# Two transformer blocks on one core: paced attention units, the renormalised residual on GpSimd, and feature turns ahead of the squares

## Time and profile before

| | us |
|---|---|
| median of 3 (range) | 2647.72 (2647.49 to 2649.39) |
| the profiled execution | 2649.36 |
| its span | 2647.6 |
| TensorE busy | 2628.9 |
| VectorE busy | 1698.8 |
| ScalarE busy | 1155.3 |
| GpSimd busy | 7.4 |

### The profile page before, as it was taken

How to read it: one execution, slowest core, us unless ns; L and a number is a source line. 1 busy time by engine, 2 the same in 40 slices (tenths; PEclk the granted TensorE clock), 3 DMA queues, 4 the chain that set the end, 5 groups by cost and what they waited for, 6 DMA issues and landing times.

```text
span 2647.6 us, 34571 instructions
## 1 busy us (share of the span) xinstructions
PE 2628.9 (99%) x12676; PEld 2209.8 (83%) x12676; DVE 1698.8 (64%) x2521; ACT 1155.3 (44%) x1549; POOL 7.4 (0%) x43
## 2 busy tenths in 40 slices
PE   9999999999999999999999999999999999999999
PEld 7978888888878888888888888888888888888887
DVE  7668764566767555655565687877755555555555
ACT  5333444534344444444444644454444444444443
POOL 0000000000000000000000000000000000000000
PEclk9999999999999999999999999999999999999999
DMA  7545556555545556655566566544566555555555
GB/s 229 180 153 173 152 160 222 191 191 174 186 141 185 191 188 189 194 191 188 189 194 207 177 199 183 155 139 144 163 198 191 190 190 190 190 190 190 190 190 167
DMA packets 262501, 483.67 MB, mean 183 GB/s; under 512 B 17738, under 2 KB 39172, under 8 KB 262020
## 3 DMA queue, kind: packets, MB, share of 16 engines
q1 hardware_dynamic: 262372, 482.37, 57.4%
q10 hardware_dynamic: 32, 0.01, 0.0%
HBM read 480.22 MB, written 2.10 MB: 182 GB/s over the span
## 4 chain that ended last, share of the span: by engine, by line
PE 95%; DVE 3%; ACT 1%; issue 0%; DMA 0%; SPq 0%; ACTq 0%; DVEq 0%
PE bank L1087 26%; PE bank L1089 25%; PE bank L1088 25%; PE bank L1045 4%; PE bank L1048 4%; PE bank L1046 4%; PE bank L1175 2%; PE bank L1138 1%; DVE w_split L1257 1%; PE bank L1208 1%; PE bank L1191 1%; PE bank L1185 0%; PE bank L1210 0%; ACT act_junk L845 0%; ACT w_split L859 0%
## 5 line engine op out<-in xcount | busy, mean ns | idle before, releaser
L859 ACT ACTIVATE w_split<-w_raw 128x1024 fp32r<-128x1024 f32 (+2 forms) x920 | 960.7, 1046 | 1226.1 <-PE bank L1089 977.9
L1257 DVE TENSOR_TENSOR w_split<-w_raw,w_split 128x1024 fp32r<-128x1024 f32 (+2 forms) x920 | 1088.4, 1203 | 431.0 <-ACT w_split L859 422.0
L1087 PE MATMUL bank<-w_split,act_a 128*128 128x512 f32 (+2 forms) x1888 | 738.1, 391 | 3.7 <-DVE w_split L1257 2.5
L1089 PE MATMUL bank<-w_split,act_a 128*128 128x512 f32 (+2 forms) x1888 | 724.0, 383 | 0.0
L1088 PE MATMUL bank<-w_split,act_a 128*128 128x512 f32 (+2 forms) x1888 | 722.8, 383 | 0.0
L1087 PE MATMUL bank<-w_split,act_b_hi 128*128 128x512 f32 x1240 | 485.8, 392 | 1.3 <-issue 1.0
L1089 PE MATMUL bank<-w_split,act_b_lo 128*128 128x512 f32 x1240 | 482.9, 389 | 0.0
L1088 PE MATMUL bank<-w_split,act_b_hi 128*128 128x512 f32 x1240 | 482.6, 389 | 0.0
L1087 PEld LDWEIGHTS bank<-w_split,act_a 128*128 128x128 f32 x1888 | 354.7, 188 | 70.6 <-DVE w_split L1257 3.5
L1089 PEld LDWEIGHTS bank<-w_split,act_a 128*128 128x128 f32 x1888 | 354.4, 188 | 67.7
L1088 PEld LDWEIGHTS bank<-w_split,act_a 128*128 128x128 f32 x1888 | 354.9, 188 | 63.6
(11 more groups left out here) (209 smaller groups left out, 1238.8 us busy)
## 6 DMA issues: line engine op xcount, KB each, us to landing
w_raw<-in_w_ff SPq DMA_DIRECT2D x256, 512.0 KB, 4.0
w_raw<-in_w_in SPq DMA_DIRECT2D x208, 512.0 KB, 3.8
w_raw<-in_w_gate SPq DMA_DIRECT2D x88, 512.0 KB, 4.1
w_raw<-in_w_up SPq DMA_DIRECT2D x88, 512.0 KB, 4.5
w_raw<-in_w_down SPq DMA_DIRECT2D x88, 512.0 KB, 4.6
w_raw<-in_w_out SPq DMA_DIRECT2D x64, 512.0 KB, 4.4
w_raw<-in_w_in SPq DMA_DIRECT2D x24, 368.0 KB, 3.3
w_raw<-in_w_dsa_o SPq DMA_DIRECT2D x16, 512.0 KB, 4.9
```

Source lines behind the costliest of these rows:

```text
L859: nc.scalar.activation(whi[:, s, 0:w], raw[:, s, 0:w], ACT.Copy).then_inc(hi_ready, 1)
L1087: pe.matmul(o, x_hi, rhs_hi, start=k == 0, stop=False)
L1089: ins = pe.matmul(o, x_lo, rhs_hi, start=False, stop=k == c["kt"] - 1)
L1257: v_e.tensor_tensor(wlo[:, s, 0:w], raw[:, s, 0:w], whi[:, s, 0:w].bitcast(F32), ALU.subtract).then_inc(lo_ready, 1)
```

## The change

The change has three parts.

1. A new function `paced_attention` stands in for `attention` in DSA, MoBA and FoX (the memory attention keeps the old one), and `nsa_attention` has the new order too. A unit's steps are now [P of u-2, S of u, O of u-3] in one place and [N of u] by itself in the next.
2. The four `renorm` steps go from VectorE to GpSimd: for each half of the tokens one multiplication by the row factor and one by the gains. GpSimd waits for all norms so far and for the gains, with the first of them alone. A new step `renormed`, at the second chunk of `vf`, makes VectorE wait for all four.
3. In the weaves of `mo[2]` and `mo[3]` the turns `hf[0:2]` and `hf[2:4]` come ahead of the squares, which puts them one group earlier.

```diff
--- before.py
+++ after.py
@@ -168,21 +168,36 @@
     return out, values
 
 
-def nsa_attention(units):
+def paced_attention(units):
 
     out, m, values = [], len(units), []
-    for i in range(m + 1):
-        one, two = [], []
-        if i >= 1:
-            one.append(("N", units[i - 1]))
-            two.append(("P", dict(unit=units[i - 1], slot=(i - 1) % 3)))
+    for i in range(m + 3):
+        one = []
+        if 2 <= i < m + 2:
+            one.append(("P", dict(unit=units[i - 2], slot=(i - 2) % 3)))
         if i < m:
             one.append(("S", units[i]))
-        if i % 3 == 1 and i > 1:
-
-            values.append(("O", dict(units=units[i - 4:i - 1], slots=[0, 1, 2], k=8 + i // 3 - 1)))
-            two.insert(0, values[-1])
-        out += [x for x in (one, two) if x]
+        if i >= 3:
+            values.append(("O", dict(units=[units[i - 3]], slots=[(i - 3) % 3], k=units[i - 3]["k"])))
+            one.append(values[-1])
+        out += [one] + ([[("N", units[i])]] if i < m else [])
+    return out, values
+
+
+def nsa_attention(units):
+
+    out, m, values = [], len(units), []
+    for i in range(m + 2):
+        one = []
+        if i % 3 == 2 and i > 2:
+
+            values.append(("O", dict(units=units[i - 5:i - 2], slots=[0, 1, 2], k=8 + i // 3 - 1)))
+            one.append(values[-1])
+        if i >= 2:
+            one.append(("P", dict(unit=units[i - 2], slot=(i - 2) % 3)))
+        if i < m:
+            one.append(("S", units[i]))
+        out += [one] + ([[("N", units[i])]] if i < m else [])
     values.append(("O", dict(units=units[m - 3:m], slots=[0, 1, 2], k=8 + m // 3 - 1)))
     out.append([values[-1]])
     return out, values
@@ -240,13 +255,13 @@
     seq += weave(qa[1])
     seq += weave(vb[1], index[16:18] + [turns(qa[1], "qa", 4, scale=SCALE)] + index[18:], 2)
     dsa = [dict(kind="dsa", q="qa", kk="ka", v="va", h=h, kh=h, k=h) for h in range(8)]
-    steps, o_dsa = attention(dsa)
+    steps, o_dsa = paced_attention(dsa)
     part = cut(steps, 2)
     qb = [w_in(QB + i * CH, "rope", rows=True) for i in range(2)]
     seq += weave(qb[0], part[0], 1)
     seq += weave(qb[1], [turns(qb[0], "qb", 0, scale=SCALE)] + part[1], 2)
     moba = [dict(kind="moba", q="qb", kk="kb", v="vb", h=h, kh=h, k=8 + h) for h in range(8)]
-    steps, o_moba = attention(moba)
+    steps, o_moba = paced_attention(moba)
     part = cut(steps, 4)
     part[0] = [turns(qb[1], "qb", 4, scale=SCALE)] + part[0]
     for i in range(4):
@@ -284,7 +299,7 @@
     (half0, half1), (half2, half3) = groups_of(mo[0]), groups_of(mo[1])
     seq += steps[3][1:] + steps[5][1:] + steps[4][1:] + steps[5][:1] + steps[6][::-1] + steps[7] + [half0, half2] + steps[8] + steps[9] + [half1, ("E", mo[0]), half3, ("E", mo[1])]
     hf = [turn("x", 2 * i * P, "A", 2 * i, mo[i // 2], gain="g_ff") for i in range(8)]
-    seq += weave(mo[2], [squares(0, mo[0]), hf[:2]], 1) + weave(mo[3], [squares(1, mo[1]), squares(2, mo[2]), hf[2:4]], 1)
+    seq += weave(mo[2], [hf[:2], squares(0, mo[0])], 1) + weave(mo[3], [hf[2:4], squares(1, mo[1]), squares(2, mo[2])], 1)
     pend = [hf[4:6], squares(3, mo[3]), hf[6:]]
 
 
@@ -362,7 +377,7 @@
     steps, o_nsa = nsa_attention(units)
     part = cut(steps, 6, NSA_SHARES)
     seq += weave(vf[0], [("gates", {})] + part[0] + [tq], 2)
-    seq += weave(vf[1], cum + part[1], 1)
+    seq += weave(vf[1], [("renormed", {})] + cum + part[1], 1)
     pend = []
     late = []
     for m, (name, col, i, gain, scale) in enumerate((("qf", QF, 0, "fox_q_norm_2", SCALE), ("kf", KF, 0, "fox_k_norm_2", None),
@@ -371,7 +386,7 @@
         seq += weave(c, part[2 + m][:2] + late + part[2 + m][2:] + pairs(pend), 1)
         pend = turns(c, name, 4 * i, hgain=gain, scale=scale)
         late = [("E", c)]
-    steps, o_fox = attention([dict(kind="fox", q="qf", kk="kf", v="vf", h=h, kh=h, k=h) for h in range(8)])
+    steps, o_fox = paced_attention([dict(kind="fox", q="qf", kk="kf", v="vf", h=h, kh=h, k=h) for h in range(8)])
 
     part = cut(late + steps[:4] + pairs(pend) + steps[4:], 4, (2, 5, 5, 5))
     for i in range(4):
@@ -629,6 +644,7 @@
         scores_done, row_max_ready, exp_done, probs_ready = map(sem, ("scores_done", "row_max_ready", "exp_done", "probs_ready"))
         squared, head_squared = sem("squared"), sem("head_squared")
         weighted, weighted_squared, cmp_out = sem("weighted"), sem("weighted_squared"), sem("cmp_out")
+        renormed = sem("renormed")
         scored, cmp_probs_hi = sem("scored"), sem("cmp_probs_hi")
         consts_ready, alibi_ready = sem("consts_ready"), sem("alibi_ready")
         angle_ready, sine_ready = sem("angle_ready"), sem("sine_ready")
@@ -805,11 +821,27 @@
                         else:
                             step(ins)
 
-            past = [0]
+            past, rstds = [0], [0]
 
             def visit(kind, what, turn):
                 if kind == "G":
                     past[0] = what["g"] + 1
+                elif kind == "rstd":
+                    rstds[0] += 1
+                elif kind == "renorm":
+
+                    m = what["m"]
+                    if m == 0:
+                        pool.wait_ge(rstd_ready, rstds[0])
+                        pool.wait_ge(gain_landed, 16)
+                    for t in range(NT):
+                        x = xres[:, t, m * CH:(m + 1) * CH]
+                        ins = nc.gpsimd.tensor_scalar(x, x, s_("rstd_f", t, t + 1), None, ALU.mult)
+                    step(ins)
+                    for t in range(NT):
+                        x = xres[:, t, m * CH:(m + 1) * CH]
+                        ins = nc.gpsimd.tensor_tensor(x, x, gain_rows[:, m * CH:(m + 1) * CH], ALU.mult)
+                    ins.then_inc(renormed, 1)
                 elif kind == "distances":
                     if what["part"] == 0:
                         wait(pool, lo_ready, past[0])
@@ -1689,13 +1721,8 @@
                         v_e.tensor_scalar(s_("half_h"), s_("rstd_h"), 0.5, None, ALU.mult).then_inc(rstd_ready, 1)
                     else:
                         v_e.memset(s_("t1", 0, 1), 0.0).then_inc(rstd_ready, 1)
-                elif kind == "renorm":
-                    ahead()
-                    m = what["m"]
-                    for t in range(NT):
-                        x = xres[:, t, m * CH:(m + 1) * CH]
-                        ins = v_e.scalar_tensor_tensor(x, x, s_("rstd_f", t, t + 1), gain_rows[:, m * CH:(m + 1) * CH], ALU.mult, ALU.mult)
-                    step(ins)
+                elif kind == "renormed":
+                    dve.wait_ge(renormed, 4)
                 elif kind == "blocks":
                     ahead()
                     blocks(what)
```

## The result

| | us |
|---|---|
| kernel before, 8 runs beside it | 2647.86 (2647.49 to 2651.16) |
| kernel after, 8 runs | 2655.87 (2654.55 to 2656.22) |
| ratio, 95% interval | 1.0025 [1.0017, 1.0034] |
| the profiled execution after, its span | 2655.96, 2654.2 |

The change made the kernel slower: by 8.0 us as the difference of the two medians, by 6.6 us as the ratio has it (4.5 to 9.0). The forecast was +1.7, 2649.4, and its range ended at +6.8, 2654.5; the nearest rival was B with +6.4, 2654.1. The runs of the kernel before fall into groups about 1.7 us apart: those with a mean granted clock of 1.000 take about 2648.1, those with 0.999 mostly 2649.6 to 2650. The profiled one of before was of the second group, so a difference of traces and a difference of medians can be 1.7 apart.

What follows compares the result with a forecast made beforehand. TensorE, busy 2628.9 of 2647.6 us, was taken as the bound, so only its waits could be won. Attention order -0.6, feature turns -2.7 and GpSimd residual +5 gave +1.7 on the median: 2649.4 us, range 2641.5 to 2654.5.

Steps and rivals of the forecast that it cites:

- rival B: Each GpSimd operation blocks one VectorE operation in full from 1534: -3.3 + 8 + 1.7 (clock) = +6.4, 2654.1 us; chance 0.20.
- Two signs: VectorE's low-half subtractions of 1.9 us and more at 1534 to 1556; TensorE waits over 5 us in sum at 1548 to 1562.
- The 1.25 us of the earlier trace: One VectorE subtraction starting during a GpSimd cast took 1.25 us against 1.21 to 1.23: GpSimd holding VectorE seen only as 0.03.
- The other 14 are 8 x 1.0 + 6 x 0.68 = 12.1 us: GpSimd's residual operations beside VectorE's SBUF work, from 1533: two-input priced 1.0 us, one-input 0.68, scaled from a 0.51 cast.
- the lateness of 6.8 us at 1554: VectorE's delay by GpSimd: 12.1 less 1.4 beside PSUM reads, 1.8 idle and 14 x 0.15 not held.
- The next step: VectorE idles 0.87 us at 1554; its chain then runs to 1561.6, where TensorE already waits 1.48, so lateness passes through.
- 5.9 worked out and 5 taken: Cost of GpSimd's residual work to TensorE: 5.9 us, between 3.3 and 8.8 by two-input price (0.68 or 1.36); 5 taken.
- point of decision: Full blocking of VectorE by GpSimd from 1534 decides as soon as GpSimd's two-input operation takes over 1.2 us.
- Edit 3: -2.7: Feed-forward's entry, feature turns ahead of squares: 1.0 us from a shorter wait, 1.7 if the clock holds; ends 0 and -3.9.
- Edit 1: -0.6: New attention order: gains together 2.6 us, losses together 2.0, sum -0.6; ends -5.3 and +3.
- The losses: Attention: O6 waits for O5's bank, 0.7 us each in DSA and fox; DSA turn at 291.67 loses 0.6 more; together 2.0.
- Only 0.8 of this goes: NSA, TensorE's 1.72 us wait at 1738.43: only 0.8 us gained, since the late head norm stays ahead of N on VectorE.

Runs made afterwards that it cites:

- e8: Kernel before plus two one-input and two two-input GpSimd multiplications of 128x512 at 1.5 us, before VectorE has work; multiplication by a row factor took 1.58 us.
- e2: Kernel before with only the renormalised residual moved to GpSimd: 2660.18 us against 2648.99, ratio 1.0043.
- e3: Kernel before with only the feature turns put ahead of the squares: 2647.10 us against 2648.99, ratio 0.9994.
- e7: Kernel before with the feature turns ahead of the squares and the new order in NSA attention only: 2643.04 us against 2649.76, ratio 0.9977.
- e4: Kernel before with only the new attention order (paced_attention and the new nsa_attention): 2647.14 us against 2648.99, ratio 0.9993.

## Why the prediction was too low

**Edit 2, the step that failed.** Its mechanism held. GpSimd's operations and VectorE's SBUF operations hold each other up, and not one way only: low halves took 1.57 instead of 1.22, while VectorE's reads of PSUM kept their time, and GpSimd's multiplication by the row factor took up to 3.28 against 1.58 alone. Two signs came as foretold: the longest low half took 2.31 us (1.9 and more), and TensorE's waits between 1548 and 1562 sum to 5.3 (over 5). The 1.25 us of the earlier trace rows overlapped only the last 0.18 us of the cast, and was no measure of the price. By the Trainium skill, "SBUF — State Buffer", section "SBUF: two separate sides", the edit had to cost time; the trace agrees, with 10.3 us more on VectorE.

The words that failed are "The other 14 are 8 x 1.0 + 6 x 0.68 = 12.1 us", and the lateness of 6.8 us at 1554 that came from it. The operation that ended at 1554.35 before (the last split of a compressed block) comes 8.16 us later (1561.82 against 1553.66), and TensorE and VectorE had come into the stretch 1.73 early: 9.9 us late. The price of 0.68 was read from a cast of 128x384; the multiplication by a row factor, alone, takes 1.58 (`e8`). With the measured 1.28 and 1.58 the same sum would have been 8 x 1.28 + 6 x 1.58 = 19.7, less 5.3 of deductions, 14.4, and that is too much: GpSimd bears a part of the waiting itself (29.2 us busy against 8 x 2.86 = 22.9 at these shortest durations). The next step, less 0.87 of idle time, held: the head norm's chain started at 1556.36 before and 1563.69 after, 7.33 + 1.73 = 9.06 late, and so did TensorE's matmul, 1561.67 and 1568.99, 9.05. That is the share of VectorE, against 5.9 worked out and 5 taken, the last step down without a reason given.

The second term left out is the clock. The forecast had none for edit 2; rival B had 1.7. Behind the matmul of 1568.99 the difference grows by 1.4 us in the stretch granted at 0.60, and by 1.6 in another near 1645: 2.9. With 9.05 it is the 12.0 of the trace. What ran at the lower level before 1568.99 cost nothing more, since TensorE would only have waited longer for the same low half. `e2` agrees (clock 0.997 to 0.998 in all five runs), but the 1.6 near 1645 is no sure part of edit 2: it stands behind a wait of 1.94 us that the kernel before has too (1638.81), and `e3` and `e7` have such a stretch there.

Rival B was the nearest: it had the clock, and 8 us for the port. Its point of decision, a two-input operation of over 1.2 us, was passed (1.28), but the one-input operation is the dearer one, and that stood in no case. Taking 5 out of 3.3 to 8.8 leaned to the side of the price with the weaker row behind it.

**Edit 3: -2.7, measured -2.8 in the traces at this place, -1.2 at full clock, -1.9 by medians.** The wait is 0.72 where 1.1 was expected, and the clock held (1.00 at 790 to 800): 1.1 and 1.7. The step that made this a gain of the median was wrong: about half of the runs of the kernel before have, by their mean clock, no drop at all. And the drop seems to move rather than go. The profiles with the old entry (before, `e2`, `e4`, `e8`) all have it at 797 to 799, and one of them (`e2`) has another at 1650. Of the six with the new one, four have a drop between 1636 and 1648 instead. With edit 3 alone 6 of 11 runs have clock 1.000, and 13 of 27 of the kernel before: too few to tell from no gain of the clock.

**Edit 1: -0.6, measured -2.3 at full clock.** The losses were about right. P6, O5, P7, O6 in one slot, TensorE after, and the same once more at 1869 (the slot's excess over its parts is 0.95 and 0.93, with 0.7 expected):

```profile
311.71 0.55 PE L1223 MATMUL bank<-ident,s_sb 128*128 128x128 f32 x3
312.76 0.48 PE L1240 MATMUL bank<-pt_sb,heads 128*128 128x256 f32 x1 [0.50 <-DVE act_b_lo L1660]
```

and the DSA turn, which waited 0.49 and was to wait 0.6 more:

```profile
291.06 1.06 PE L1207 MATMUL bank<-ident,stage 128*128 128x128 f32 x8 [0.95 <-DVE stage L1304]
```

What was too small is the gain in NSA, 3.9 against 2.1. "Only 0.8 of this goes", for the wait of 1.72 at 1738.43, was wrong. VectorE before, then VectorE and TensorE after, at the same unit:

```profile
1736.22 1.21 DVE L1257 TENSOR_TENSOR w_split<-w_raw,w_split 128x1024 fp32r<-128x1024 f32 x1
```

```profile
1742.55 1.29 DVE L1326 TENSOR_TENSOR stage<-bank,small 128x512 f32<-128x512 f32 x2
1743.76 0.15 DVE L1581 RECIPROCAL small<-small 128x2 f32<-128x2 f32 x1
```

```profile
1745.03 0.49 PE L1223 MATMUL bank<-ident,s_sb 128*128 128x128 f32 x3
```

The norm does stay ahead of N, but in the kernel before a low half (1736.22, 1.21 us) stood between the two; now N comes right behind the norm, and the transpose waits for nothing. The offset falls by 1.9 us here, 1.1 more than the 0.8. The other 0.7 us that NSA gained beyond the forecast are not put to single waits here.

## What to carry to other kernels

Work moved to GpSimd while VectorE is on the path isn't free where both work in SBUF: price it as time taken from VectorE, with the operation's own duration, and measure that form alone first (`e8` shows it in four rows) instead of scaling a cheaper one. That is an upper bound: here VectorE lost 10.3 us to operations that last 22.9 at their shortest, and GpSimd waited for the rest of the collisions itself. Look where it will land: from its only wait on, it ran in the stretch in which VectorE had hardly any idle time, and at another place it cost 4 to 5 us less. Before a clock drop is counted as a gain to be had, look at the mean clocks of the other runs, and at whether another wait of the same length stands behind it.

## What was not expected of the hardware

- GpSimd's multiplication of 128x512 float32 by a factor for each row takes 1.56 to 1.58 us, its multiplication of two tiles 1.04 (one tile twice) to 1.28.
- VectorE's float32 cast within SBUF, with one input, is held by GpSimd too: 427 ns to 737 on average. The prediction counted on operations with two inputs alone. The Trainium skill, "SBUF — State Buffer", section "SBUF: two separate sides", names a float32 copy within SBUF beside them, and the trace agrees for this cast.
- The same wait of TensorE is followed by a stretch at the 1.2 GHz level in one execution and not in another. Behind the kernel's first 10 us and before its end, the ten profiles have 15 such stretches, of 3.4 or 6.8 us each, and each begins during a TensorE wait of 1.91 us or more, or at most 1.3 us behind one. Six other waits, of 1.94 to 2.11 us, have none behind them. What decides is left open.
